# A 127-row copy as two DMAs, and a LayerNorm ahead of a token shift, in a hybrid decoder step

## What is computed

```python
proj = rmsnorm(x, norm_mix_g) @ w_in            # 1024 -> 1792 (group A) + 1024 (group B)
# group A, RWKV-7: token shift, then low-rank decay, rate and gate, then the delta state
prev_rows = concatenate([shift_prev[:, None, :], pa[:, :-1]], axis=1)
xm = pa + (prev_rows - pa) * mu
r, k, v, wl, al, gl = split(xm, A_SPLITS)
w = -softplus(-(w0 + tanh(wl) @ w2)) - 0.5
a = sigmoid(a0 + al @ a2); g = sigmoid(gl) @ g2
# group B, gMLP: u, v = halves of gelu; per-group LayerNorm on v; u * (tril(W_s) vn + b)
vn = (vg - mean) * rsqrt(var + LN_EPS) * ln_g + ln_b
x = x + concat(A, B) @ w_out
x = x + peer_ffn(rmsnorm(x, norm_ffn_g))        # 8 heads x 16 experts a token, from tables of 16384 rows
x = x + (p @ ple_w) * sigmoid(rmsnorm(x) @ ple_gate_w)
```

## Time and profile before

| | |
|---|---|
| median of 3 runs | 4624.03 us |
| profiled execution, own time | 4615.67 us |
| its span | 4613.9 us |
| busy PE / DVE / ACT / POOL | 78% / 55% / 19% / 51% |
| moved by DMA | 1390.59 MB, 301 GB/s over the span |
| granted PE clock, mean | 0.89 |

### The profile page before, as it was taken

How to read it: one execution, slowest core, us unless ns; L and a number is a source line. 1 busy time by engine, 2 the same in 40 slices (tenths; PEclk the granted TensorE clock), 3 DMA queues, 4 the chain that set the end, 5 groups by cost and what they waited for, 6 DMA issues and landing times.

```text
span 4613.9 us, 42693 instructions
## 1 busy us (share of the span) xinstructions
PE 3585.8 (78%) x14690; PEld 2207.8 (48%) x14690; DVE 2542.9 (55%) x5603; ACT 899.5 (19%) x2202; POOL 2343.3 (51%) x2110
## 2 busy tenths in 40 slices
PE   4745987599868998599858998599866988857757
PEld 3733564356534654356534654356533654323414
DVE  1561748275836575275826575275735666365732
ACT  1210312032112112032112112031112112111112
POOL 1011746276646656375636656375545755454641
PEclk8877998799988999799988999799988999988878
DMA  7135889699987999789977899789986999979964
GB/s 224 49 107 201 328 319 331 223 362 348 381 297 276 341 379 358 257 306 345 366 282 279 331 385 359 257 305 334 359 289 254 345 383 347 344 263 346 371 255 170
DMA packets 554196, 1390.59 MB, mean 301 GB/s; under 512 B 39913, under 2 KB 274697, under 8 KB 553986
## 3 DMA queue, kind: packets, MB, share of 16 engines
q0 software_dynamic: 297216, 1082.26, 63.1%
q1 hardware_dynamic: 256770, 305.61, 19.5%
HBM read 1366.88 MB, written 13.56 MB: 299 GB/s over the span
## 4 chain that ended last, share of the span: by engine, by line
PE 53%; DMA 20%; DVE 17%; issue 4%; ACT 3%; SPq 2%; POOL 1%; DVEq 0%; PEldq 0%; ACTq 0%
PE peer_acc L718 23%; PE bank L737 11%; DMA wbuf<-in_w_in_dram 7%; PE bank L842 6%; PE bank L819 5%; DMA proj_s<-pa 5%; DMA wbuf<-in_peer_wq_dram 4%; DVE uring L1220 4%; PE bank L686 2%; DVE feat L1412 1%; DMA wbuf<-in_w_out_dram 1%; SPq L375 1%; DVE feat L1409 1%; DVE e L1415 1%; PE bank L930 1%
## 5 line engine op out<-in xcount | busy, mean ns | idle before, releaser
L718 PE MATMUL peer_acc<-vring,dg 128*128 128x512 f32 x4096 | 1963.3, 622 | 233.1 <-ACT dg L1013 156.6
L657 POOL DMA_INDIRECT vring<-in_peer_v_dram,eidx x1024 | 1147.8, 1121 | 1501.4 <-PE peer_acc L718 1295.0
L647 POOL DMA_INDIRECT uring<-in_peer_u_dram,eidx x1024 | 1168.0, 1141 | 683.9 <-issue 308.5
L718 PEld LDWEIGHTS peer_acc<-vring,dg 128*128 128x128 f32 x4096 | 767.4, 198 | 1105.2 <-issue 911.4
L1220 DVE CUSTOM_DVE_ANT_0 uring<-uring,px 128x1024 f32<-128x1024 f32 x1024 | 1226.6, 1220 | 36.1 <-DMA uring<-in_peer_u_dram,eidx 16.9
L737 PE MATMUL bank<-wbuf,xT 128*128 128x256 f32 (+1 forms) x2288 | 568.6, 406 | 386.7 <-DMA wbuf<-in_w_in_dram 369.0
L737 PEld LDWEIGHTS bank<-wbuf,xT 128*128 128x128 f32 (+1 forms) x2288 | 430.3, 190 | 569.1 <-issue 478.3
L1013 ACT ACTIVATE dg<-ident,qa 128x128 f32<-128x128 f32 x1024 | 325.3, 389 | 644.0 <-DVE qa L1225 628.0
L1225 DVE TENSOR_TENSOR qa<-qg,pgate 128x4 f32<-128x4 f32 x256 | 40.4, 158 | 613.5 <-ACT qg L1017 613.4
L819 PEld LDWEIGHTS bank<-xT,wbuf 128*128 128x128 f32 x2048 | 258.6, 206 | 80.6 <-issue 76.6
L819 PE MATMUL bank<-xT,wbuf 128*128 128x128 f32 (+1 forms) x2048 | 261.0, 287 | 45.3 <-DMA wbuf<-in_peer_wq_dram 41.7
(11 more groups left out here) (321 smaller groups left out, 3431.5 us busy)
## 6 DMA issues: line engine op xcount, KB each, us to landing
wbuf<-in_w_in_dram SPq DMA_DIRECT2D x91, 1024.0 KB, 10.6
wbuf<-in_peer_wq_dram SPq DMA_DIRECT2D x64, 1024.0 KB, 13.4
wbuf<-in_w_out_dram SPq DMA_DIRECT2D x32, 1024.0 KB, 8.3
wbuf<-in_ple_gate_w_dram SPq DMA_DIRECT2D x20, 1024.0 KB, 10.0
uring<-in_peer_u_dram,eidx POOLq DMA_INDIRECT x1024, 6.8
vring<-in_peer_v_dram,eidx POOLq DMA_INDIRECT x1024, 6.7
feat<-in_shift_mu_dram SPq DMA_DIRECT2D x9, 896.0 KB, 27.1
xm<-pa SPq DMA_DIRECT2D x8, 889.0 KB
```

Source lines behind the costliest of these rows:

```text
L647: gp.indirect_dma_start(uring[:, c % NU, :], None, peer_u, bass.IndirectOffsetOnAxis(ap=eidx[:, i % 2, k:k + 1], axis=0)).then_inc(sig(f"u ...
L657: gp.indirect_dma_start(vring[:, c % NV, :], None, peer_v, bass.IndirectOffsetOnAxis(ap=eidx[:, i % 2, k:k + 1], axis=0)).then_inc(sig(f"v ...
L718: last = mm(acc[half][:, :], dg[:, (c // UNIT) % 2, c % UNIT, :], vring[:, c % NV, half * 512:(half + 1) * 512], start=(c % HK == 0), stop ...
```

## The change

The copy of 127 rows is issued as two DMAs, of rows 0 to 111 and 112 to 126, on the same queue and the same semaphore, whose waits count three DMAs a block instead of two. In the list of stages the four LayerNorm stages go ahead of `shift0`, and the programs of DVE and ACT are put in that order. Nothing else is changed; the weights of the stages are the same, so the expert steps between `win10` and `lora_mm` are the same in number and are dealt out over the new order.

```diff
+SPLIT = 112
...
-SHIFT_STAGES = (["shift0", "shift1", "shift2", "lora"] + NORM("ln") + ["lora_mm", "kk", "gmlp"])
+SHIFT_STAGES = (NORM("ln") + ["shift0", "shift1", "shift2", "lora", "lora_mm", "kk", "gmlp"])
...
-                    sp.dma_start(xm[1:P, :], pa[0:P - 1, :]).then_inc(sig("prev_loaded"), 16)
+                    sp.dma_start(xm[1:SPLIT + 1, :], pa[0:SPLIT, :]).then_inc(sig("prev_loaded"), 16)
+                    sp.dma_start(xm[SPLIT + 1:P, :], pa[SPLIT:P - 1, :]).then_inc(sig("prev_loaded"), 16)
...
+                yield "ln_root"
+                sqrt_of(i + 1, "ln", st[0:n, 16:24], st[0:n, 24:32], scale=1.0 / HD, bias=eps[0:n, 1:2])
                 yield "lora"
...
-                yield "ln_root"
-                sqrt_of(i + 1, "ln", st[0:n, 16:24], st[0:n, 24:32], scale=1.0 / HD, bias=eps[0:n, 1:2])
                 yield "lora_mm"
...
+                yield from group_norm("ln", i + 1, n, uv[0:n, DA:D], uv[0:n, DA:D], "cmlp_ln_g", "cmlp_ln_b")
+                ve.sem_inc(sig("vn_ready"), 1)
+
                 yield "shift0"
-                ve.wait_ge(sig("prev_loaded"), 32 * i + (32 if prompt else 16))
+                ve.wait_ge(sig("prev_loaded"), 48 * i + (48 if prompt else 16))
...
                 yield "shift2"
                 tt(xm[0:n, :], xm[0:n, :], pa[0:n, :], ALU.add).then_inc(sig("xm_ready"), 1)
-
-                yield from group_norm("ln", i + 1, n, uv[0:n, DA:D], uv[0:n, DA:D], "cmlp_ln_g", "cmlp_ln_b")
-                ve.sem_inc(sig("vn_ready"), 1)
```

## The result

The changed kernel takes 4442.62 us (median of 4 runs, 4435.53 to 4449.86) against 4627.03 us for the kernel before on the same chip (4623.56 to 4630.86): a ratio of 0.9601, 95% interval 0.9581 to 0.9622. That is 184 us less, where 259 were forecast; 4442.6 lies just above the upper end of the range. The profiled execution took 4438.74 us (span 4437.0), its mean granted PE clock was 0.902.

What follows compares the result with a forecast made beforehand. The prediction took the 127-row copy on one engine, delaying SP's later loads and so PE, to bound the kernel. Split -280, block 0 -27, order +48 made -259 us: 4624.03 to 4365 us, range 4310 to 4440.

Steps and rivals of the forecast that it cites:

- What bounds the kernel: Blocks 1 to 7: one engine carries the 127-row copy in 61 us, holding SP; chunk 9 is issued 22 us late.
- The split: Copy as 112 and 15 rows: win10 ends 40 us sooner in each of seven blocks, 280 us gained.
- Its normal landing is 10.6 us on: Block 2, chunk 9 issued at win7's end, 851.6: 10.6 us plus 5.0 us for copy and `mu`, landing at 867.
- gathers stop when PE stops: Argument against a full DMA delaying chunk 9: the share was 0.43 and 0.06 while PE awaited that chunk.
- rival 1: Chunk 9 lands as late after its issue as now, in an already full stretch: 4470 us, chance 0.12.
- Win9 takes 3.7 instead of 5.87 us: Block 2, PE's win9: as fast as win10 now, since PE's clock has not been at 0.50 for 30 us.
- The order: LayerNorm ahead of the shift: `uv` to `lora_mm` 23 us against 17.3, 6 us lost in blocks 1 to 8, 48 us.
- Block 0: No experts; LayerNorm runs in idle time, copy and `mu` land by 75, `lora_mm` starts at 88.5: 27 us gained.
- rival 4: Both copy parts stay on one engine; order loses 8 x 6, wins 2 us in block 0: 4670 us, chance 0.05.
- The sum: Whole kernel: -280 - 27 + 48 = -259 us against the median of 4624.03, giving 4365 us.

## Why the prediction was off

**What bounds the kernel: right.** One engine carried the copy, SP stood behind it, and chunk 9 stood behind SP. 113 rows bring it all back; 112 rows take it away.

**The split: mechanism right, its delay sized too small.** The store takes 0.84 us, chunk 9 goes out right behind win7, `proj_s<-pa` leaves the chain, 15 rows cost nothing that shows. The step that failed is "Its normal landing is 10.6 us on; ahead of it now go copy and `mu`, 1.8 MB, at 364 GB/s 5.0 us". That is 15.6 us; 23.5 were measured in block 2, 21.3 to 25.2 in all seven. Both of its terms were too small. Copy and `mu` were ahead for up to 10.6 us (810.38 to 821), not 5.0: 364 GB/s was what the whole core moved, and SP's queue had 136 GB/s of it beside the gathers. Chunk 9 itself then took some 13 us, not 10.6, on a queue that got one packet for each of the gathers' and about a quarter of their bytes. With copy and `mu` behind it, it took 7.6 us from its issue, so their place ahead of it costs 15.3 us, at three times the 5.0. The argument that "gathers stop when PE stops", with which rival 1 was set aside, failed with it. POOL did stop:

```profile
823.95 0.94 POOL L649 DMA_INDIRECT uring<-in_peer_u_dram,eidx  x1 [0.30 <-issue]
843.04 0.94 POOL L659 DMA_INDIRECT vring<-in_peer_v_dram,eidx  x1 [18.15 <-PE peer_acc L720]
```

But it had issued six gathers of U and six of V since 801, and what was not yet moved of its gathers, 4.02 MB from 821 on, kept the engines full (share 1.04, 395 GB/s) until chunk 9 was there.

The second, smaller part is "Win9 takes 3.7 instead of 5.87 us, as win10 does now, since PE's clock has not been at 0.50 for 30 us". It took 6.46. PE stopped at 821.66. The granted clock was still 1.00, 2.4 GHz, up to 825, and 0.50, 1.2 GHz, from 827 to 838, so most of win9 (834.05 to 840.51) ran at the lower level. This stall cost its own length and, behind it, some 2.8 us on the next chunk. Counted in block 2, from the copy's issue: chunk 9 on hand 6.6 us later than forecast (33.6 against 27.0), win9 2.8 longer, win10's end 2.0 sooner behind it: some 7.5 us. Seven times that is 52, the difference between 280 and the measured 228.

**Rival 1** was the nearest: it had the right cause (a stretch that is already full), but took all of it. Its 28 to 33 us would have given 175; 23 us gave 228.

**The order: sign right, size low.** From `uv` to `lora_mm` 23 us were forecast for 17.3; block 2 took 24.1, the seven blocks 47 more instead of 7 x 6 = 42, and the sample 5 (24.1 against 18.8). PE's wait at the transposes is there, 4.75 us, and DVE's at L1252, 25.24 us. Not forecast was the step behind it: in blocks 2 and 7 the way from `lora_mm` to `sms` is 3.5 us longer (34.0 against 30.5), the third column's 8 us; why was not tried. 47 + 5 + 8 = 60 instead of 48; the medians say 61 (order alone) and 63 (the changed kernel run again, over the split alone).

**Block 0: size right, one reason wrong.** 27 us were forecast, 29 came, but the split alone has them too: LayerNorm in the idle time, which the forecast counted in, adds nothing. The order alone moves this point by 2 to 3 us, as rival 4 had it (2 us).

The start of block 0 after the change (ACT's last `uv`, LayerNorm, the shift, `lora_mm`; all engines), against the earlier trace rows:

```profile
69.31 0.38 ACT L993 ACTIVATE uv<-bank 128x256 f32<-128x256 f32 x1 [3.61 <-PE bank L739]
...
69.78 0.69 DVE L1252 TENSOR_REDUCE st<-uv 128x8 f32<-128x512 f32 x1 [45.84 <-ACTq L1047]
...
75.83 2.02 DVE L1287 TENSOR_TENSOR xm<-xm,pa 128x1792 f32<-128x1792 f32 x1 [0.25 <-DVE uv L1263]
...
86.48 0.69 DVE L1297 TENSOR_TENSOR feat<-bank,p_rwkv_w 128x512 f32<-128x512 f32 x1 [4.50 <-PE bank L779]
```

The copies are there before LayerNorm is done (the shift waits 0.25 us, and for DVE itself); `lora_mm` starts at 86.48 where 88.5 was forecast.

**The sum.** 228 + 29 - 60 = 197 us by the rows, 184 and 190 by the medians of the two comparisons; the rest is within the spread of the stretches that no edit touches (16 us between two profiles of after). 52 of the 259 were lost on chunk 9 and 12 on the order, and block 0 gave 2 more than forecast.

## What to carry to other kernels

When a transfer is freed from a slow neighbour, price its landing by the share that its own queue gets of the DMA, as a window by queue shows it, and not by the rate of the whole core. Where both queues had work all the time they got packets about one for one here, so the queue with the smaller rows got the fewer bytes. Then look at what still goes ahead of it on its queue, and put what is needed later behind it (here worth over 80 us: 4442.62 and 4436.15 to 4353.84). Of two edits in one change, run each alone: here one gave 260 us (4632.98 to 4372.93 on one chip) and the other took over 60 of them back. Work that waits for nothing belongs in a wait that is there anyway: the shift cost nothing while it lay ahead of win10's result.

## What the runs showed of the hardware

- One row decides: 112 + 15 rows against 113 + 14 is 4442.62 against 4663.11 us, and 0.84 against 25.08 us for the issue behind the first DMA.
- A copy inside SBUF of 0.91 MB ahead of chunk 9, beside the broadcast, delays the end of win10 by 6.9 us; the broadcast of 0.92 MB from HBM, beside the copy, by 3.7. Why the copy weighs twice as much was not tried.
- On a full DMA the queue with the one load that PE stood still for had the smaller part: 4.50 MB in 33 us, against 7.05 MB of POOL's gathers, for which DVE and PE had no wait over 1 us in that time. From 821 to 834 us the two queues moved 1104 and 1105 packets, with 1.11 and 4.02 MB; in the 13 us ahead of chunk 9's landing in block 7, 1102 and 1103; in those of blocks 3 to 6, 1142 to 1285 and 1052 to 1099. These counts look as if the engines took the queues in turn; it was not tried with rows of another size.
